# Reordering the splits and waits around attention, the first projection and the first group of a float32 transformer backbone

## The reference, cut to what matters

```
mod_x = (silu(c) @ w_mod[i] + b_mod[i]).reshape(-1, N_MOD, D_MODEL)
hx = modulate(rmsnorm(x, norm1_w[i]), mod_x[:, 0], mod_x[:, 1])     # hc the same for ctx
if i % 2 == 0: yx, yc = ssd_mixer(hx, hc, ssd_w_in, ..., ssd_w_out) # in: z, x, B, C, dt
else:          yx, yc = window_attention(hx, hc, w_qkv, b_qkv, sink, w_o, b_o, cos, sin, ...)
x = x + mod_x[:, 2][:, None] * yx
h = modulate(rmsnorm(x, norm2_w[i]), mod_x[:, 3], mod_x[:, 4])
f = swiglu(h, w1, w3, w2)  or  moe_swiglu(h, router, w1, w3, w2)
x = x + mod_x[:, 5][:, None] * f
```

## Time and profile before

| | before |
|---|---|
| median of 3 runs | 2188.5 us |
| the profiled execution, its own time | 2185.93 us |
| its span in the profile | 2184.0 us |
| TensorE busy | 2097.4 us (96%) |
| VectorE busy | 1488.5 us (68%) |
| ScalarE busy | 1209.0 us (55%) |
| mean granted TensorE clock | 0.981 of full |
| chain that ended last | TensorE 87%, VectorE 6%, ScalarE 3% |

### The profile page before, as it was taken

The page is one execution under the profiler, slowest core; times in us unless marked ns, Lnnn a source line. Parts: engine busy times, 40 slices in busy tenths (PEclk is TensorE's granted clock), DMA queues, the critical chain, the costliest instruction groups (busy, mean ns, idle before and its releaser), DMA issues.

```text
span 2184.0 us, 26866 instructions
## 1 busy us (share of the span) xinstructions
PE 2097.4 (96%) x11254; PEld 1690.4 (77%) x11254; DVE 1488.5 (68%) x1433; ACT 1209.0 (55%) x1258; POOL 72.5 (3%) x20
## 2 busy tenths in 40 slices
PE   7899999899899999988989999999999999999997
PEld 4788888777677777867667888888888888888885
DVE  3688888853333232235648879888887988888796
ACT  4656666632422222243647676667677676677764
POOL 0111122100000000000000000000000000000000
PEclk9999999999999999989989999999999999999999
DMA  8234544422344444224127989898999989899992
GB/s 317 99 135 168 189 166 163 183 77 99 131 157 161 180 161 162 97 79 145 71 105 265 366 342 352 337 359 334 367 347 342 360 336 354 339 367 348 342 359 80
DMA packets 71776, 510.08 MB, mean 234 GB/s; under 512 B 7968, under 2 KB 8352, under 8 KB 10976
## 3 DMA queue, kind: packets, MB, share of 16 engines
q1 hardware_dynamic: 71568, 508.15, 61.6%
q10 hardware_dynamic: 80, 0.13, 0.0%
HBM read 504.97 MB, written 3.28 MB: 233 GB/s over the span
## 4 chain that ended last, share of the span: by engine, by line
PE 87%; DVE 6%; ACT 3%; issue 2%; DMA 1%; SPq 0%; POOL 0%; DVEq 0%; ACTq 0%; POOLq 0%
PE ps L1106 14%; PE ps L1104 14%; PE ps L1105 14%; PE ps L661 12%; PE ps L663 11%; PE ps L662 11%; PE ps L780 2%; PE ps L1088 1%; PE ps L1135 1%; PE ps L673 1%; DVE area L1904 1%; DMA d_raw<-in_dense 1%; PE ps L1168 1%; DVE area L1881 1%; DVE area L1911 1%
## 5 line engine op out<-in xcount | busy, mean ns | idle before, releaser
L2185 DVE TENSOR_TENSOR w_lo<-w_raw,w_hi 128x2048 fp32r<-128x2048 f32 x336 | 748.2, 2286 | 46.8 <-ACT w_hi L1585 46.8
L1585 ACT ACTIVATE w_hi<-w_raw 128x2048 fp32r<-128x2048 f32 x336 | 624.4, 1916 | 71.3 <-PE ps L1106 70.1
L1711 DVE TENSOR_TENSOR d_lo<-d_raw,d_hi 128x2048 fp32r<-128x2048 f32 (+1 forms) x76 | 171.9, 2261 | 312.3 <-ACT d_hi L1291 312.3
L1104 PE MATMUL ps<-w_hi,x_hi 128*128 128x512 f32 x896 | 357.2, 399 | 1.1 <-DVE x_lo L2241 1.1
L1106 PE MATMUL ps<-w_hi,x_lo 128*128 128x512 f32 x896 | 355.1, 396 | 0.0
L1105 PE MATMUL ps<-w_lo,x_hi 128*128 128x512 f32 x896 | 350.7, 391 | 0.0
L1291 ACT ACTIVATE d_hi<-d_raw 128x2048 fp32r<-128x2048 f32 (+1 forms) x76 | 143.9, 1893 | 370.7 <-DMA d_raw<-in_dense 232.6
L661 PE MATMUL ps<-h_top,d_hi 128*128 128x512 f32 (+1 forms) x816 | 327.5, 401 | 22.1 <-DVE h_low L1703 10.6
L663 PE MATMUL ps<-h_top,d_lo 128*128 128x512 f32 (+1 forms) x816 | 319.8, 392 | 0.0
L662 PE MATMUL ps<-h_low,d_hi 128*128 128x512 f32 (+1 forms) x816 | 315.6, 387 | 0.0
L661 PEld LDWEIGHTS ps<-h_top,d_hi 128*128 128x128 f32 x816 | 156.1, 191 | 65.7 <-issue 18.8
(11 more groups left out here) (296 smaller groups left out, 2495.0 us busy)
## 6 DMA issues: line engine op xcount, KB each, us to landing
w_raw<-in_experts SPq DMA_DIRECT2D x336, 1024.0 KB, 4.8
d_raw<-in_dense SPq DMA_DIRECT2D x120, 1024.0 KB, 5.7
area<-acum_rows SPq DMA_DIRECT2D x16, 1024.0 KB, 7.2
d_raw<-in_dense SPq DMA_DIRECT2D x4, 768.0 KB, 4.6
xT<-in_xt SPq DMA_DIRECT2D x4, 512.0 KB, 6.8
gate_rows<-area SPq DMA_DIRECT2D x4, 512.0 KB, 6.8
hT<-gate_rows SPq DMA_DIRECT2D x2, 1024.0 KB, 6.0
cst<-in_consts SPq DMA_DIRECT2D x2, 512.0 KB, 12.7
```

What stands on the lines that cost most here:

```text
L1104: mm(o, hi, w_hi[u % HIGH][:, a:a + 512], start=first, stop=False)
L1585: A(w_hi[n % HIGH][:], w_raw[n % RAW][:], ACT.Copy).then_inc(S["whi_done"], 1)
L1711: TT(d_lo[u][:, 0:w], d_raw[u][:, 0:w], d_hi[si % D_HIGH][:, 0:w].bitcast(F32), ALU.subtract)\
L2185: TT(w_lo[n % RAW][:], w_raw[n % RAW][:], w_hi[n % HIGH][:].bitcast(F32), ALU.subtract)\
```

## The change

1. SyncE issues x(0) after two `m0` units instead of four.
2. TensorE's first scores wait for six ropes instead of ten; the v tiles are waited for ahead of the second scores, the tenth rope ahead of `turn(0)` (which writes the banks that the last ropes read) and of scores 12.
3. ScalarE: in group 0 the two `evac_raw` and `token_evac` come ahead of `segments_back`. The high part of wo unit 1 (W0+49) comes behind the masks' copies.
4. VectorE: the low part of wo unit 1 moves from ahead of the v tiles to behind `maxima(1)`; that of wo unit 3 (W0+51) moves from ahead of the residual additions to behind the fourth.

```
-            for n in range(4):
-                load_dense(n)
+            load_dense(0)
+            load_dense(1)
             load_dense(D_AT[EARLY])
+            load_dense(2)
+            load_dense(3)
...
-            pe.wait_ge(S["q_out"], 10)
-            pe.wait_ge(S["v_out"], 4)
+            pe.wait_ge(S["q_out"], 6)
...
+                if i == 1:
+                    pe.wait_ge(S["v_out"], 4)
+                if i == 12:
+                    pe.wait_ge(S["q_out"], 10)
...
+                if i == 0:
+                    pe.wait_ge(S["q_t1"], 10)
...
+                if g == 0:
+                    evac_raw(1, 0)
+                    evac_raw(1, 1)
+                    token_evac(0)
+                    segments_back(0)
+                    segments_forth(0)
...
-            dense_high(W0 + 49)
             act.wait_ge(S["band_in"], 32)
...
+            dense_high(W0 + 49)
...
-            dense_low(W0 + 49)
             dv.wait_ge(S["bv_in"], 16)
...
                 maxima(i)
+                if i == 1:
+                    dense_low(W0 + 49)
...
-            dense_low(W0 + 51)
             for k in range(KT):
+                if k == 4:
+                    dense_low(W0 + 51)
```

More of the change, by code:

```diff
@@ L1448, in _ @@
                 dense_high(3 * g + 4)
[L1449 to L1453, removed]
+                if g == 0:
[4 more added lines that the diff above has]
+                    segments_forth(0)
+                else:
+                    segments_back(g)
+                    evac_raw(g + 1, 0)
+                    evac_raw(g + 1, 1)
+                    segments_forth(g)
+                    token_evac(g)
                 row_exps(g)
```

## The result

The changed kernel took 2172.73 us (median of 4 runs, 2170.22 to 2173.71), the kernel before beside it 2187.82 (4 runs). The ratio is 0.9929, with a 95% interval of 0.9917 to 0.994. Predicted were 2172.5 and 2167.0 to 2178.0. The profiled execution took 2173.24 us with a span of 2171.1; TensorE's share rose from 96% to 97%.

A forecast was written before the change was run, and what follows sets the result against it. The prediction took TensorE, busy for 96% of the span, as the bound, its long waits also costing half clock. Terms 7.7 + 6.6 + 1.1 + 0.6 = 16.0 us off 2188.5 gave 2172.5 us, range 2167.0 to 2178.0.

The forecast's parts named there:

- Output projection, 7.7: Between wo units 1 and 2: 5.7 us of wait and 2.1 of clock saved, less 0.1; bounds 7.0 to 7.9.
- Attention's start, 6.6: Value tiles and first scores start earlier, so turn(2) begins at about 1043.1 against 1049.70; bounds 4.1 and 7.9.
- the lower bound: Attention's start: gain of only 4.1 us if the new pauses let the clock fall, costing 3.2 us at most.
- Group 0, 1.1: Outputs can start 3.5 us earlier, less 2.4 us for half clock behind a new wait.
- TensorE's bc(1) follows the transposes with no wait: Group 0: once ScalarE's copies come first, bc(1) runs straight behind the transposes, 6.5 us earlier.
- the forecast wait of 5 us ahead of the outputs: Group 0: TensorE arrives at 110.5 and idles about 5 us until outputs(0) can start at 115.5.
- The beginning, 0.6: x(0) lands earlier, first product at about 28.2 instead of 31.02; middle taken between 2.1 gained and -0.9 with half clock.
- (a): Rival: half clock follows all three new pauses (beginning, group 0, ahead of turn(0)); gain 10.9, time 2177.6 us; chance 0.13.
- (b): Rival: the clock stays up and the wait is simply gone everywhere; gain 20.4, time 2168.1 us; chance 0.08.
- (c): Rival: attention never gets its full clock, up to 50 us lost against 16 gained, 2222 us; chance 0.02.
- (d): Rival: attention's first maximum is held by something else, 6.6 becomes 2; gain 11.4, time 2177.1 us; chance 0.07.

The follow-up runs named there:

- e6: The changed kernel with SyncE's old order at the start put back: 2169.66 us, ratio 0.9917.
- e8: The kernel before with only TensorE's three waits at attention's start changed, the splits left in place: 2183.12 us, ratio 0.9984.
- e9: The kernel before with only the split of wo unit 1 moved on ScalarE and VectorE, TensorE's waits unchanged: 2182.8 us, ratio 0.9985.
- e7: The changed kernel with 15 unused products put ahead of three waits of the first projection, to hold the clock: 2171.38 us, ratio 0.9926.
- e2: The kernel before with only ScalarE's reordering in group 0: 2185.96 us, ratio 0.9986.
- e5: The changed kernel with GpSimd's first mask waiting until VectorE has done that group's 16 convolution steps: 2167.73 us, ratio 0.9906.
- the repeat: The changed kernel as it is, run once more as yardstick, against the kernel before: 2170.75 us, ratio 0.9921.
- e13: The changed kernel with VectorE's low part of the first group's next raw unit ahead of its four steps at L1904: 2170.3 us, ratio 0.993.
- e1: The kernel before with only the start changed, x(0) issued after two m0 units: 2189.63 us, ratio 1.0003.
- e4: The kernel before with only the low part of wo unit 3 moved behind the fourth residual addition: 2179.42 us, ratio 0.9959.

## Why the prediction was right

**Output projection, 7.7.** Measured 7.7 in every profile that holds the edit. Unit 2's first matmul starts 0.13 us behind the end of unit 1's last, and its matmuls with unit 3's take 11.6 us at clock 1.00, as forecast; the low part of unit 3 begins at 1109.50, once k = 3 is done, and is in time.

**Attention's start, 6.6.** Measured 6.4 to 6.5, and 6.9 in e6. Value tiles at the product's end, two scores under the ropes, a pause of 2.07 us ahead of the first turn, maxima(2) behind the low part: each step is in the rows above. The third turn starts at 1044.83 against 1049.70 in the earlier trace rows, 4.87 earlier with TensorE 1.6 late by then. e8 and e9 show that the waits and the move were both needed. What the lower bound priced too high is the clock: the half clock did follow the pause, and where up to 3.2 us were feared it cost 0.5 (6.4 with it, 6.9 without it in e6), since VectorE's low part held up the third maxima anyway.

**Group 0, 1.1 with bounds 0 and 3.5.** Measured 3.2 to 3.4 (2.2 and 1.3 in e6 and e7). The step that failed is "TensorE's bc(1) follows the transposes with no wait". Its low part stands behind segments(0) on VectorE (97.30 to 99.58), so the forecast wait of 5 us ahead of the outputs was paid as 3.14 us ahead of bc(1), and the half clock with it (0.56 from 99.7 to 103.6 us). TensorE's work ahead of the outputs ended at 117.10, the states at 117.13, and the outputs started at 117.23, so VectorE's 3.5 us came through nearly whole. That was a close thing, and partly luck. In e2, e5 and the repeat, too, the outputs started within 0.3 us of the states' end; but in e6 and e7, with the half clock twice as long (and in e7 the longer wait), the states were done 1.3 and 2.1 us before TensorE got to the outputs, and the gain fell to 2.2 and 1.3. In the case that was assumed, which e13 made, the half clock cost 1.7 instead of the forecast 2.4, and 1.7 instead of 1.1 were left as gain.

**The beginning, 0.6 with bounds -1.0 and 4.7.** The first product of x(0) starts at 28.18 as forecast (28.2), the second piece at 42.37, not at 40. The execution lost 1.6, outside the lower bound: the last mod unit's pause of 1.41 us was followed by 6.8 us at clock 0.52, and its weights came 0.6 later than forecast (38.8, not 38.2): the fifth unit landed at 26.3 instead of 25.7, so the last transfer was issued at 28.3 instead of 27.3, and was in flight for 10.4 us. Five other profiles of the new order gain 0.3 to 2.6, those of the old order lie between +0.2 and -2.1. The medians (e1, e6) see nothing.

**The sum.** The terms measured at their places are 3.3 + 6.4 + 7.7 = 17.4 and about nothing for the start, against 16.0; the whole by medians is 15.1 and, repeated, 17.3. The 2.2 us missed in group 0 and the start's 0.6 partly cancel, so the total was closer than its terms, and that the median came within 0.3 us of 2172.5 is luck: the four runs lie 3.5 us apart, and the stretches without an edit move by as much. Of the rivals, (a) came true in its condition and not in its price: in this profile all three new pauses were followed by half clock (0.52, 0.56 and 0.74 in the stretches above), but it took less in group 0 and attention than (a) has. (b) fell because the clock did take something, (c) because attention kept the pace of before from the third turn on (no difference arises between 1050 and 1107 us in any profile), (d) because the first maximum came at 1035.34, 5.1 us before its old stamp with TensorE 1.6 us late by then.

**What stays open.** Why the stretches to 1030 and behind the output projection differ by 2 to 4 us between executions of kernels equal there was not tried. Where the differences arise can be seen: at matmuls which one execution ran at half clock and the other did not (448 to 460 us, behind waits of 2.1 to 3.3 us; 1136 to 1153 us). In the column "rest", before ran at 0.50 from 1136.2 to 1143.0 and from 1149.9 to 1153.3, and e4 and e8, which have -4.4 and -4.3, at 1.00 in both. What decides it in an execution no run here shows.

## What to carry to other kernels

Removing a wait moves it to the next input that is late: list for the work that is pulled ahead every operand and where its producer stands on its own engine, not only the one that the old wait named. A pause of TensorE with its half clock is free only as long as another engine's chain is longer up to their next meeting, so put the pause there and not behind, and count on the longer half clock: in group 0 the shorter one used up all the slack, and the profiles with the longer one lost 1 to 2 us. And before a 2 us difference between two profiles is believed, look at the same stretch in kernels that don't hold the edit.

## What the runs showed of the hardware

- VectorE's convolution step (128x512, two SBUF inputs) and GpSimd's mask (128x2048) can't run side by side. Alone the mask takes 2.01 us; beside the steps 5.1 to 6.4 with VectorE undisturbed (it ends about 1.9 us behind the last step of the row); or 2.0 to 2.6 with one step at 2.5 instead of 0.75. Which it is changes from group to group and from execution to execution of one kernel.
- A pause of 1.4 us between short products was followed by the half clock in one execution (0.52 from 38.7 to 45.5 us) and not in another (1.00 in e13). The instructions there were the same; the three pauses were 0.78, 1.42 and 1.41 us in the first and 0.20, 1.41 and 1.42 in e13.
- The half clock behind one and the same wait differed in length: in group 0, behind 3.59 us in e6, it was granted from 95.1 to 101.9 us; behind 3.60 us in the changed kernel's repeat, from 97.0 to 100.4.
